# The second block's output projection, moved by token tiles into the rounds of the recurrent tiles

## The reference

```python
x = x + 0.5 * swiglu(rms_norm(x, ffn_norm[l, 0]), ...)
p = rms_norm(x, mix_norm[l]) @ w_in[l]
pa, pb, pc = split_cols(p, GROUP_SPLITS)
ya = dsa_attention(pa, ...)                  # 512 wide
yb, v_first = rwkv7_time_mix(pb, ...)        # 256 wide, a recurrence over the tokens
yc = gated_deltanet(pc, ...)                 # 256 wide, another one
x = x + jnp.concatenate([ya, yb, yc], axis=-1) @ w_out[l]
x = x + 0.5 * swiglu(rms_norm(x, ffn_norm[l, 1]), ...)
```

## Time and profile before

| | us |
|---|---|
| median of 3 runs (3974.7 to 3976.48) | 3976.01 |
| the profiled execution | 3974.07 |
| its span (first to last instruction) | 3972.1 |
| busy: PE | 3720.4 (94%) |
| busy: PEld (PE's weight loads) | 3075.4 (77%) |
| busy: DVE | 1382.0 (35%) |
| busy: ACT | 1415.5 (36%) |
| busy: POOL | 1321.6 (33%) |
| mean granted TensorE clock | 0.955 |

### The profile page before, as it was taken

One profiled execution on the slowest core, in us unless ns is written; L12 is line 12 of the kernel. 1 busy time (PEld: TensorE's weight loads), 2 busy tenths in 40 slices (PEclk: granted clock), 3 DMA queues, 4 the chain that ended last, 5 costly groups with the idle time before them and its releaser, 6 DMA issues.

```text
span 3972.1 us, 54526 instructions
## 1 busy us (share of the span) xinstructions
PE 3720.4 (94%) x23108; PEld 3075.4 (77%) x23108; DVE 1382.0 (35%) x2982; ACT 1415.5 (36%) x2426; POOL 1321.6 (33%) x631
## 2 busy tenths in 40 slices
PE   8987999998889989999998789999999999779999
PEld 7876888887678878888766678888888866668887
DVE  2345111334531132112666741112111486752111
ACT  3444222335432233223445432223222455424221
POOL 3101544420144434444311124444444321114443
PEclk9988999998799999999998899999999999879999
DMA  4101333320122323333210023333333310003332
GB/s 121 48 11 53 100 97 93 100 65 17 38 85 91 110 94 91 102 101 88 70 38 2 2 66 100 113 98 93 93 106 96 85 52 12 2 28 91 95 101 91
DMA packets 406643, 291.85 MB, mean 73 GB/s; under 512 B 18017, under 2 KB 356865, under 8 KB 406401
## 3 DMA queue, kind: packets, MB, share of 16 engines
q1 hardware_dynamic: 400832, 284.17, 24.1%
q10 hardware_dynamic: 5136, 2.96, 0.4%
q0 software_dynamic: 432, 1.25, 0.1%
HBM read 286.24 MB, written 2.10 MB: 73 GB/s over the span
## 4 chain that ended last, share of the span: by engine, by line
PE 82%; DVE 10%; ACT 6%; issue 1%; POOL 0%; DMA 0%; SPq 0%; DVEq 0%; ACTq 0%
PE ps L714 13%; PE ps L716 13%; PE ps L715 13%; PE ps L832 7%; PE ps L835 7%; PE ps L834 7%; PE ps L886 2%; PE ps L1350 2%; PE ps L903 1%; PE ps L894 1%; PE ps L965 1%; PE ps L741 1%; PE ps L1060 1%; PE ps L1061 1%; PE ps L1062 1%
## 5 line engine op out<-in xcount | busy, mean ns | idle before, releaser
L3008 POOL TENSOR_TENSOR wl<-wraw,wh 128x1024 fp32r<-128x1024 f32 (+2 forms) x532 | 1245.8, 2342 | 2324.4 <-ACT wh L2396 2324.4
L2396 ACT ACTIVATE wh<-wraw 128x1024 fp32r<-128x1024 f32 (+2 forms) x532 | 548.1, 1032 | 1092.5 <-PE ps L835 588.5
L714 PE MATMUL ps<-x_T,wh 128*128 128x512 f32 (+1 forms) x2336 | 894.2, 383 | 0.0
L716 PE MATMUL ps<-x_T,wl 128*128 128x512 f32 (+1 forms) x2336 | 892.0, 382 | 0.0
L715 PE MATMUL ps<-x_T,wh 128*128 128x512 f32 (+1 forms) x2336 | 891.9, 382 | 0.0
L714 PEld LDWEIGHTS ps<-x_T,wh 128*128 128x128 f32 x2336 | 439.3, 188 | 85.7 <-issue 1.0
L716 PEld LDWEIGHTS ps<-x_T,wl 128*128 128x128 f32 x2336 | 439.2, 188 | 85.1
L715 PEld LDWEIGHTS ps<-x_T,wh 128*128 128x128 f32 x2336 | 439.3, 188 | 84.6 <-issue 0.5
L832 PE MATMUL ps<-wh,h_T 128*128 128x512 f32 x1056 | 411.5, 390 | 0.0
L835 PE MATMUL ps<-wh,h_T 128*128 128x512 f32 x1056 | 410.9, 389 | 0.0
L834 PE MATMUL ps<-wl,h_T 128*128 128x512 f32 x1056 | 410.8, 389 | 0.0
(11 more groups left out here) (748 smaller groups left out, 5277.8 us busy)
## 6 DMA issues: line engine op xcount, KB each, us to landing
wraw<-in_ffn_w_gate_dram SPq DMA_DIRECT2D x88, 512.0 KB, 3.8
wraw<-in_ffn_w_up_dram SPq DMA_DIRECT2D x88, 512.0 KB, 3.8
wraw<-in_w_in_dram SPq DMA_DIRECT2D x82, 512.0 KB, 3.8
wraw<-in_ffn_w_down_dram SPq DMA_DIRECT2D x80, 512.0 KB, 3.7
wraw<-in_w_gate_dram SPq DMA_DIRECT2D x44, 512.0 KB, 3.8
wraw<-in_w_up_dram SPq DMA_DIRECT2D x44, 512.0 KB, 3.8
wraw<-in_w_down_dram SPq DMA_DIRECT2D x40, 512.0 KB, 3.7
wraw<-in_w_o_dram SPq DMA_DIRECT2D x16, 512.0 KB, 3.7
```

What stands on the lines that cost most here:

```text
L714: mm(b[:, t0:t1], wh[:, k, :], xTh[:, k, t0:t1], k == 0, False)
L716: ins = mm(b[:, t0:t1], wl[:, k, :], xTh[:, k, t0:t1], False, k == 7)
L2396: copy(hl_of(w)[0], raw_of(w)).then_inc(*s.sig("w", "hi", w))
L3008: tt(wl, raw_of(w), wh.bitcast(F32), ALU.subtract).then_inc(*g.sig("w", "lo", w))
```

## The change

The attention half of `mix` (columns 0 to 511) is complete when the DSA work is through, and tile j of the other half when `rec_tile` j is. A new generator `out_lane` of 67 steps goes one step per round beside the recurrent tiles after `over()`; what it has left runs after them.

- Attention half (r = 0): eight passes, one per column half of `w_out` and token tile, one every four rounds: four transposes (`turn`), the split by ACT and DVE, in each of four rounds three matmuls (`piece`), and the sum added to `x_tm` by DVE (`close`). The same tile is transposed and split again for the second column half. The split halves lie in `h_T`.
- Recurrent half (r = 1): tiles 0, 1 and 2 begin at rounds 36, 40 and 53, one transposition and split per tile, six matmuls a round in four rounds, two closes, then the norm of the tile (two gains, mean, root, inverse, scale).
- `w_out` is cut in two row halves by two column halves, two pieces for each; six of the split stages (ACT copy and POOL subtraction) a layer run in the rounds, at 0, 16, 18, 32, 34 and 36. The last lies in `h_T` outside the ring, and ring slots are counted without it.
- `Stock` loses the six half buffers of `wraw`, gets one in `con`, and gets four of its sixteen later ones at round 35.
- After the barrier stand only tile 3 of the recurrent half, its norm, and `halves_F` with three weights in place of two; SP no longer waits at the barrier for the loads.
- Root and square no longer alternate as often on ACT: two loads of its tables less.

```diff
@@ -156,8 +156,9 @@
         f(w, l, 1352, 256)
         f(w, l, 2248, 768)
         f(w, l, 1608, 512)
-        for half in range(2):
-            t("w_out_2", l, 0, 8, half * 512, 512)
+        for r in range(2):
+            for half in range(2):
+                t("w_out_2", l, r * 4 * P, 4, half * 512, 512)
         ffn("ffn_w_gate_2", "ffn_w_up_2", "ffn_w_down_2", 2 * l + 1)
     return out
...
-def mixer_rounds(heads, unit, index, top, project, gates, tiles, masks, over):
+def out_lane(take, turn, split, piece, close, chunk, norm, give):
+
+    for t in range(67):
+        if t == 0:
+            take()
+        if t in (0, 16, 18, 32, 34, 36):
+            chunk()
+        for a in range(8):
+            half, j, n = a // 4, a % 4, t - 4 * a
+            if 2 <= n < 6:
+                piece(0, half, j, (n - 2,))
+            if n == 6:
+                close(0, half, j)
+            if n == 0:
+                turn(0, half, j)
+            if n == 1:
+                split(0, half, j)
+        if t == 35:
+            give()
+        for j, first in enumerate((36, 40, 53)):
+            n = t - first
+            if 2 <= n < 6:
+                piece(1, (n - 2) // 2, j, (2 * (n % 2), 2 * (n % 2) + 1))
+            if n in (5, 7):
+                close(1, (n - 5) // 2, j)
+            if n == 0:
+                turn(1, 0, j)
+            if n == 1:
+                split(1, 0, j)
+            if 8 <= n < 13:
+                norm(j, n - 8)
+        yield
...
@@ -374,6 +411,8 @@
     over()
     clear.append(True)
     for _ in chain:
+        next(out, None)
+    for _ in out:
         pass
 
...
+        fourth = [where["w_out_2", l, 512] for l in range(2)]
+        ring = [w for w in range(len(weights)) if w not in fourth]
+        slot = {w: n % NHL for n, w in enumerate(ring)}
+        before = {w: ring[n - NHL] for n, w in enumerate(ring) if n >= NHL}
...
                 self.free = [(spare[:, i * 512:(i + 1) * 512], (("w", "used", w),)) for i in range(16)]
-                self.free += [(x[:, a:a + 512], (("w", "lo", w + AHEAD),)) for x in wraw for a in (0, 512)]
-                self.late = [(x, tuple(("dsa over", l, q) for q in ENG)) for x in extra + [s[:, :] for s in scr]]
+                self.free.append((con[:, N2:N2 + 512], ()))
+                self.late = [(x, tuple(("dsa over", l, q) for q in ENG)) for x in extra[4:] + [s[:, :] for s in scr]]
...
+            def output(l, stock):
+
+                ws = []
+
+                def take():
+                    ws.extend(use() for _ in range(8))
+                    for q in ENG:
+                        pe.wait_ge(*at("dsa over", l, q))
+
+                def turn(r, half, j):
+                    b, free = bank(("oT", l, r, half, j), ("out", "lo", l, r, half, j))
+                    pe.wait_ge(*free)
+                    if r:
+                        pe.wait_ge(*at("rec", "mixed", l, j))
+                    for k in range(4):
+                        ins = tr(b[:, k * P:(k + 1) * P], mx[:, j, r * 512 + k * P:r * 512 + (k + 1) * P])
+                    ins.then_inc(*pe.sig("out", "t", l, r, half, j))
+
+                def piece(r, half, j, ks):
+                    oh, ol = out_Ts[j] if r else out_T0[j % 2]
+                    if ks[0] == 0:
+                        pe.wait_ge(*bank(("out", l, r, half, j), ("out", "x", l, r, half, j), hold=True)[1])
+                        pe.wait_ge(*at("out", "lo", l, r, 0 if r else half, j))
+                    b = psum[book.bank[("out", l, r, half, j)]]
+                    for k in ks:
+                        w = ws[4 * r + 2 * half + k // 2]
+                        wh, wl = hl_of(w)
+                        o = slice(k * P, (k + 1) * P)
+                        pe.wait_ge(*at("w", "lo", w))
+                        mm(b[:, :], oh[:, o], wh[:, k % 2, :], k == 0, False)
+                        mm(b[:, :], oh[:, o], wl[:, k % 2, :], False, False)
+                        ins = mm(b[:, :], ol[:, o], wh[:, k % 2, :], False, k == 3)
+                        if j == 3 and k == 1:
+                            ins.then_inc(*pe.sig("w", "used", w))
+                    if ks[-1] == 3:
+                        ins.then_inc(*pe.sig("out", "p", l, r, half, j))
+                        if j == 3:
+                            pe.also("w", "used", w)
+
+                def close(r, half, j):
+                    held.discard(book.bank[("out", l, r, half, j)])
+
+                def give():
+                    stock.put(pe, l, *extra[:4])
+
+                return out_lane(take, turn, split=nothing, piece=piece, close=close, chunk=nothing, norm=nothing,
+                                give=give), turn, piece, close
...
+                             [rec_tile(l, j, stock) for j in range(4)], masks, over, lane)
                 barrier("o", l)
-                to_T(("out", l), mx, lambda j, c: ("bar", "o", l, "dve"))
-                proj_T(8, 512, xTh, xTl, lambda j: ("T", "lo", ("out", l), j, 1), early=2)
                 rms = (("rms", l, 2), mx, lambda j, c: ("rms", "x", l, 2, j))
-                proj_T(8, 512, xTh, xTl, late=3, between=partial(early_T, *rms))
-                first_F(*rms, (0, 1))
+                turn(1, 0, 3)
+                to_T(*rms, (0, 1))
+                for half in range(2):
+                    piece(1, half, 3, range(4))
+                    close(1, half, 3)
+                to_T(*rms, (2,))
+                halves_F(rms[0], 3, lambda: to_T(*rms, (3,)), 1)
                 if l == 0:
                     rms = (("rms", 1, 0), mx, lambda j, c: ("rms", "x", 1, 0, j))
-                    ffn(3, partial(early_T, *rms))
+                    ffn(3, partial(early_T, *rms), 3)
                     first_F(*rms, (0, 1))
                 else:
-                    ffn(5)
+                    ffn(5, None, 3)
...
+                gain, mean, inverse = rms_parts(l, 2)
+
+                def split(r, half, j):
+                    oh, ol = out_Ts[j] if r else out_T0[j % 2]
+                    v.wait_ge(*at("out", "hi", l, r, half, j))
+                    tt(ol, psum_of("oT", l, r, half, j)[:, :], oh.bitcast(F32),
+                       ALU.subtract).then_inc(*v.sig("out", "lo", l, r, half, j))
+
+                def close(r, half, j):
+                    xs = xtm[:, j, half * 512:(half + 1) * 512]
+                    v.wait_ge(*at("out", "p", l, r, half, j))
+                    tt(xs, xs, psum_of("out", l, r, half, j)[:, :], ALU.add).then_inc(*v.sig("out", "x", l, r, half, j))
+
+                def norm(j, n):
+                    if n == 0:
+                        gain(j, 0)
+                        gain(j, 1)
+                    if n == 1:
+                        mean(j)
+                    if n == 3:
+                        inverse(j)
+
+                def give():
+                    stock.put(v, l, *extra[:4])
+
+                def last():
+
+                    name = ("rms", l, 2)
+                    split(1, 0, 3)
+                    low(name, 0)
+                    low(name, 1)
+                    for half in range(2):
+                        close(1, half, 3)
+                        gain(3, half)
+                    mean(3)
+                    low(name, 2)
+                    inverse(3)
+                    low(name, 3)
+
+                return out_lane(nothing, nothing, split, nothing, close, nothing, norm, give), last
...
                     s.wait_ge(*at(f"w{w % NRAW}", w))
-                    if w >= NHL:
-                        s.wait_ge(*at("w", "used", w - NHL))
+                    if w in fourth:
+                        s.wait_ge(*at("rec", "b3", fourth.index(w), 3))
+                    elif w in before:
+                        s.wait_ge(*at("w", "used", before[w]))
                     copy(hl_of(w)[0], raw_of(w)).then_inc(*s.sig("w", "hi", w))
...
+                def take():
+                    for q in ENG:
+                        s.wait_ge(*at("dsa over", l, q))
+
+                def split(r, half, j):
+                    s.wait_ge(*at("out", "t", l, r, half, j))
+                    if r:
+                        s.wait_ge(*at("rec", "b3", l, 3))
+                    elif 4 * half + j > 1:
+                        s.wait_ge(*(at("out", "p", l, 0, half, j - 2) if j > 1 else at("out", "p", l, 0, 0, j + 2)))
+                    oh = (out_Ts[j] if r else out_T0[j % 2])[0]
+                    copy(oh, psum_of("oT", l, r, half, j)[:, :]).then_inc(*s.sig("out", "hi", l, r, half, j))
+
...
+                    stock.put(s, l, *extra[:4])
+
+                def last():
+
+                    split(1, 0, 3)
+                    high(name, 0)
+                    high(name, 1)
+                    use(2, True)
+                    stage(wat[0] + 2)
+                    square(3, 0)
+                    high(name, 2)
+                    square(3, 1)
+                    norm(3, 2)
+                    norm(3, 4)
```

(2 more changed lines are left out.)

83 lines of the change are left out of this document (50 added, 33 removed).

## The result

The changed kernel takes 4000.4 us (median of 4 runs, 3999.54 to 4001.62), the kernel before 3975.36 in the same comparison (4 runs): ratio 1.0064, interval 1.0046 to 1.0081. It is 25 us slower; 3964 was forecast, and the range ended at 3996. The prediction took 0.2% as what can be told from no change; this is three times that.

What follows compares the result with a forecast made beforehand. Neither PE nor DVE bounds the rounds, dependencies pass between them; PE bounds the tail. Rounds 24 + 4 + 6 + 4 + 1 - 3 = 36 us longer, tail 42 shorter, 12 us gained in all: 3976 - 12 = 3964, range 3936 to 3996.

Steps and rivals of the forecast that it cites:

- The tail: Mix transposes to two finished swiglu weights, after the rounds: some 66 us of PE work, 42 us shorter in each layer.
- Step 5: Fewer scratch buffers and PSUM banks held by the lane in the rounds: 1 us a layer, bounds 0 and 10.
- Step 1: PE's 168 matmuls and 44 transposes added to the rounds: 24 of 43.4 us a layer fall on the path.
- Step 2: Solve's 64x64 weights start late behind 128x128 ones: 12 times 0.33 us, 4 us a layer, bounds 0 and 12.
- Step 3: DVE's 31 added splits, closes and gains in the rounds: nine on the chain, 6 us a layer, bounds 4 and 12.
- Step 4: GpSimd's six subtractions in the rounds, four beside DVE stages at 1.0 us each: 4 us a layer, bounds 0 and 9.6.
- port rival: Each GpSimd subtraction in a DVE stage stops DVE from start to end: 9.6 for 4 us, 3975 us; chance 0.14.
- Step 6: Pieces fill PE in the rounds and raise its granted clock: 3 us a layer less, bounds -9 and +3.
- The nearest rival: Pieces in the rounds stand before solve matmuls, leaving idle time unused: PE term 38, 50 us longer, 3992 us; chance 0.24.

Runs made afterwards that it cites:

- e9: The kernel before with only the changed kernel's smaller scratch pool (17 buffers for 22), no lane: rounds 172.9 and 176.7 us, whole 3985.85 us.
- e7: The changed kernel with DVE and ACT doing the lane's step of a round ahead of the recurrence's, PE's order unchanged: rounds 217.0 and 219.9 us, whole 3976.09 us.
- e6: The changed kernel with three PSUM banks for the lane alone and five for the recurrence: rounds 221.7 and 227.5 us, whole 3991.28 us.
- e10: e7 with the 12 matmuls of a pass in one round, 30 groups a layer less: rounds 214.4 and 224.6 us, whole 3975.90 us.
- e1: The changed kernel with only two of the 12 matmuls of each pass in the rounds: rounds 213.1 and 219.9 us, whole 3972.28 us.
- e3: The changed kernel with DVE's splits and closes in the rounds on 64 of 512 columns: rounds 221.2 and 223.8 us, whole 3987.27 us.
- e5: The changed kernel with two of 12 matmuls a pass, DVE's splits and closes and GpSimd's subtractions narrowed: rounds 200.4 and 200.1 us, whole 3938.44 us.
- e16: e7 with two of 12 matmuls a pass, DVE's splits and closes and GpSimd's subtractions narrowed: rounds 185.2 and 191.2 us, whole 3914.49 us.
- e12: e7 with groups of 12 matmuls ahead of PE's waits for DVE, tile 2's 24 behind the last recurrence matmul: rounds 221.4 and 218.6 us, whole 3975.87 us.

## Why the prediction was wrong

- **What bounds.** Right as to the tail, which is PE's. The reading of the rounds, that neither engine bounds them and dependencies pass between the two, was right too, but I drew the wrong price from it: I costed each moved operation by where it stands and left out whom it makes wait.
- **The tail, 42 us a layer.** Right: 42.6 and 43.2.
- **Step 5, banks and buffers: 1 us, bounds 0 and 10.** This is the step that failed. The smaller pool cost nothing without the lane (e9). The order that makes PE wait for splits and closes cost 9.6 and 14.8 (e7 against the changed kernel), about half of it through shared banks (4.9 and 7.2, e6): the upper bound of 10 in layer 0, and over it in layer 1. I had counted the recurrence instructions that wait for the lane, 13 in layer 0, and then wrote that what is waited for is mostly a round old. It is a round old in the order; in time it is the last thing of DVE's round (the close at 2243.80, the solve at 2244.55), and in DVE's long rounds PE is ahead of it. The same step left out the split: a piece that waits for it holds the solve behind it.
- **Step 1, matmuls on the path: 24.** Mis-sized. 140 of the 168 matmuls cost 25.5 and 21.5; at that price all 168 with the 44 transposes come to 34 and 29 of the 43.4 us (168/140 for the matmuls, and 79% and 67% of 4.8). Nearer to the busy share (28.5) than to the share of the chain (20.5), and over both. PE's busy time rose by 55.7 and 52.1 us where 43.4 were counted: a piece among solve matmuls holds the queue longer than three matmuls in a row (2234.68 to 2235.58, 0.90 us for the 0.69 counted).
- **Step 2, changes of shape: 4.** -2.6 us for 30 groups less at the same granted clock (layer 0 of e10), some 0.1 a group where 0.33 was taken for a third of them; layer 1 (+4.7) had a lower clock and says nothing.
- **Step 3, DVE: 6 for 31 operations.** 25 of them, narrowed to an eighth, gave 2.4 and 1.1 where nothing waits for them: not more than forecast. In the changed kernel the same cut gave 5.4 and 10.9; that a shorter DVE round also makes the waits shorter would explain it, and was not measured by itself.
- **Step 4, GpSimd: 4.** 4.5 and 6.2 in the changed kernel, 3.9 and 6.1 without the waits: about right in layer 0, low in layer 1. The mechanism of the port rival is there: five of six subtractions a layer stop one DVE operation until they end. Its price of 9.6 is not, since the operation stopped starts 0.2 to 1.7 us into the subtraction and would have taken time of its own, and those on PSUM run on. What the Trainium skill says ("SBUF — State Buffer", section "SBUF: two separate sides"), that the loser fully blocks, fits L2289 and L2280; the term of 9.6 that follows if DVE is stopped from start to end does not come out.
- **Step 6, the clock: -3.** The granted clock rose from 0.87 and 0.82 to 0.90 and 0.88, as forecast. By the mean, the time at 1.2 GHz was 45 and 56 us against 45 and 64; what that is worth was not measured by itself.
- **Sum** for layer 0, from the runs: 9.6 waits + 25.5 matmuls + 2.4 DVE + 3.9 GpSimd + 12.3 rest = 53.7; layer 1: 14.8 + 21.5 + 1.1 + 6.1 + 14.7 = 58.2. The cuts were made in that order; in another, the parts would differ, as e1 and e3 show; taken last, the waits are 15.2 and 8.9 (e5 against e16). The rest of 12.3 and 14.7 holds 11.2 us of matmuls and transposes, and was not parted.
- **The nearest rival** is "slower: the pieces stand in front", given 0.24 and 3992. It had the piece ahead of the next solve matmul right, as at 2234.68, but the wait in front of it is the lane's own, for its split, and not one that the recurrence had; that wait stood in no rival, only in step 5. The rival decided from a PE term of 30 on; PE's part came to about that, and the waits added the rest. That its 50 us of longer rounds are near the 53.7 of layer 0 is in part luck.

## What to carry to other kernels

When work is interleaved into a chain that passes between two in-order engines, price the waits that it adds before the work itself: ask for each result of the new lane what stands ahead of its producer in that engine's queue, and do the lane's step first there; the same instructions were 24 us cheaper in that order. Idle time of an engine is not room by itself: behind the chain's last matmul, ahead of a wait of 8.3 us, 24 matmuls were nearly free, and spread between solve steps 67 to 79% of each was paid. Groups ahead of shorter waits in the midst of the rounds saved nothing (e12). To find what a lane costs, take its parts out only after its waits are gone; before that, waits fill part of the place of what is taken out.
